# Seven-product form: another order of the first pair's products, and five operations of a head at other places of their queues

## Time and profile before

| | us |
|---|---|
| median of 3 runs (1496.05 to 1500.35) | 1499.07 |
| time of the profiled execution | 1500.38 |
| span of its profile | 1498.7 |
| PE busy in the span | 1364.2 (91%) |
| DVE, ACT, POOL busy | 972.7, 664.5, 604.8 |

### The profile page before, as it was taken

One profiled execution on the slowest core, in us unless ns is written; L12 is line 12 of the kernel. 1 busy time (PEld: TensorE's weight loads), 2 busy tenths in 40 slices (PEclk: granted clock), 3 DMA queues, 4 the chain that ended last, 5 costly groups with the idle time before them and its releaser, 6 DMA issues.

```text
span 1498.7 us, 18769 instructions
## 1 busy us (share of the span) xinstructions
PE 1364.2 (91%) x7159; PEld 1105.7 (74%) x7159; DVE 972.7 (65%) x1637; ACT 664.5 (44%) x959; POOL 604.8 (40%) x393
## 2 busy tenths in 40 slices
PE   6898999999999999988996789899999999997897
PEld 4687887888888888877874567677776767775685
DVE  6487778878696978674357266666666666667313
ACT  6244444352535353532235345555455555546113
POOL 6443333243242333253127954445455544521120
PEclk9999999999999999999997899999999999998999
DMA  6110111101011111030222111121111112002502
GB/s 186 54 43 15 29 36 36 36 22 50 22 37 34 36 29 36 29 113 11 89 66 117 28 29 36 36 64 36 43 28 43 36 35 63 23 29 99 183 28 113
DMA packets 101660, 77.82 MB, mean 52 GB/s; under 512 B 2898, under 2 KB 92099, under 8 KB 101571
## 3 DMA queue, kind: packets, MB, share of 16 engines
q1 hardware_dynamic: 101570, 76.62, 17.0%
HBM read 59.83 MB, written 16.78 MB: 51 GB/s over the span
## 4 chain that ended last, share of the span: by engine, by line
PE 66%; DVE 19%; ACT 5%; POOL 4%; issue 3%; DMA 1%; POOLq 0%; SPq 0%; DVEq 0%; ACTq 0%; PEldq 0%
PE psum L446 27%; PE psum L574 14%; PE psum L2110 3%; DVE stick L1750 3%; DVE terms L1619 3%; PE psum L2084 3%; PE psum L2028 2%; PE psum L1973 2%; PE psum L2043 2%; PE psum L1998 2%; PE psum L2019 1%; PE psum L2097 1%; DVE soft L1743 1%; POOL acc L923 1%; PE psum L1982 1%
## 5 line engine op out<-in xcount | busy, mean ns | idle before, releaser
L446 PE MATMUL psum<-u_hi,w_hi 128*128 128x512 f32 x752 | 308.7, 411 | 24.4 <-DVE u_lo L1336 6.7
L446 PE MATMUL psum<-u_lo,w_hi 128*128 128x512 f32 x752 | 306.4, 407 | 0.0
L446 PE MATMUL psum<-u_hi,w_lo 128*128 128x512 f32 x752 | 301.6, 401 | 0.0
L416 POOL TENSOR_TENSOR w_lo<-w_raw,w_hi 128x1024 fp32r<-128x1024 f32 (+1 forms) x51 | 122.7, 2406 | 325.8 <-ACT w_hi L411 325.8
L446 PEld LDWEIGHTS psum<-u_hi,w_hi 128*128 128x128 f32 x752 | 143.5, 191 | 58.1 <-issue 16.3
L446 PEld LDWEIGHTS psum<-u_lo,w_hi 128*128 128x128 f32 x752 | 143.4, 191 | 29.8 <-issue 3.8
L446 PEld LDWEIGHTS psum<-u_hi,w_lo 128*128 128x128 f32 x752 | 143.1, 190 | 29.3 <-issue 2.2
L878 POOL TENSOR_TENSOR Lb<-dec,level 128x512 f32<-128x512 f32 (+1 forms) x64 | 89.0, 1405 | 126.3 <-PE psum L2028 69.0
L574 PE MATMUL psum<-u_hi,w_hi 128*128 128x512 f32 x256 | 107.9, 421 | 22.2 <-ACT b_raw L1246 10.1
L411 ACT ACTIVATE w_hi<-w_raw 128x1024 fp32r<-128x1024 f32 (+1 forms) x51 | 52.2, 1024 | 160.5 <-PE psum L446 104.1
L1396 DVE TENSOR_TENSOR b_raw<-b_raw,psum 128x512 f32<-128x512 f32 x80 | 54.8, 684 | 102.6 <-PE psum L574 102.0
(11 more groups left out here) (257 smaller groups left out, 3050.7 us busy)
## 6 DMA issues: line engine op xcount, KB each, us to landing
w_raw<-in_a_w_in SPq DMA_DIRECT2D x33, 512.0 KB, 4.0
w_raw<-in_b_w_in SPq DMA_DIRECT2D x16, 512.0 KB, 4.9
w_raw_b<-in_b_w_in SPq DMA_DIRECT2D x16, 512.0 KB, 4.9
x_stage<-in_x SPq DMA_DIRECT2D x8, 512.0 KB, 7.3
w_raw<-in_b_w_out SPq DMA_DIRECT2D x8, 512.0 KB, 4.0
out<-fin_o SPq DMA_DIRECT2D x8, 512.0 KB, 2.6
b_rows<-o_row SPq DMA_DIRECT2D x14, 256.0 KB, 2.2
o_raw<-b_rows SPq DMA_DIRECT2D x7, 512.0 KB, 7.1
```

The costliest lines, as they stand in the source:

```text
L416: G.tensor_tensor(tiles(w_lo, key), tiles(w_raw, key), tiles(w_hi, key).bitcast(F32), ALU.subtract).then_inc(lo_done, 1)
L446: mm = PE.matmul(psum[:, half], (w_hi, w_hi, w_lo)[part][:, n % 2, k], (u_hi, u_lo, u_hi)[part][:, k, half * HALF:(half + 1) * HALF], star ...
```

## The change

1. `FIRST_ORDER` becomes p1, p5, p2, p3, p6, p7, p4. In pair 0, p5 and p3 have the second bank and the other five the first; the waits of `pair_products` and the sums in DVE's `take_pair` follow. Inputs are made in the new order: DVE makes the remainders of p3 before `sums_t` and those of p6 after it, ACT makes the upper parts of p3 before those of p6, p7 and p4. On POOL the remainders of pair 0's and 1's weights (`factor_lo`) move ahead of some of the second half's square additions, which are dealt out between them.
2. ACT, step 0 of a head: Silu of the gate, with its wait for `gn_done`, goes from step 1 behind softplus to step 0 ahead of softplus.
3. ACT, step 6: the exponential of step 7 (128 wide) goes in after the first of the three passes of the next head's softplus, instead of behind the third.
4. DVE, step 5: `scale_qk` goes from behind `exponent` to ahead of `scan`.
5. DVE, step 7: the products that end there are taken ahead of `scan`, instead of behind `exponent`.
6. DVE, step 0: `scale_v` of the first half goes ahead of `copy_aT`.

In the last head, where no pairs follow, ACT also does the split of the first output weights ahead of Silu and that of the second behind the softplus.

```diff
-FIRST_ORDER = ("p1", "p2", "p6", "p7", "p5", "p4", "p3")
+FIRST_ORDER = ("p1", "p5", "p2", "p3", "p6", "p7", "p4")
...
-            return psum[:, (p + (name in SECOND_BANK)) % 2]
+            return psum[:, (p + (name in (SECOND_BANK if p > 0 else ("p5", "p3")))) % 2]
...
         def pair_products(p, first, last):
...
+                    if p == 0 and name in ("p1", "p5"):
+                        PE.wait_ge(proj_taken, LAST_GROUP + 2 * KB - (1 if name == "p1" else 0))
+                    elif p == 0 and name in BY_ACT + ("p6",):
+                        PE.wait_ge(pair_act, 1 if name == "p2" else 2)
+                    elif p == 0:
+                        PE.wait_ge(pair_dve, {"p3": 1, "p7": 3, "p4": 4}[name])
...
         @block.gpsimd
...
             factor_lo(3)
             input_lo("p7")
+            factor_lo(4)
             input_lo("p4")
-            factor_lo(4)
+            factor_lo(5)
+            factor_sums(1)
             add_b_squares(1, 1, 4)
-            factor_sums(1)
-            factor_lo(5)
-            add_b_squares(1, 4, KB)
             factor_lo(6)
+            add_b_squares(1, 4, 5)
+            factor_lo(7)
+            add_b_squares(1, 5, 6)
+            factor_lo(8)
+            add_b_squares(1, 6, KB)
...
         @block.scalar
...
+                elif cb == HALF_KB:
+                    input_hi("p5", HALF_KB - 1)
+                    input_hi("p3", 0)
                 else:
-                    if cb == HALF_KB:
-                        input_hi("p5", HALF_KB - 1)
-                    else:
-                        for name in ("p6", "p7"):
-                            input_hi(name, cb - HALF_KB - 1)
-            for name in ("p6", "p7"):
-                input_hi(name, HALF_KB - 1)
+                    input_hi("p3", cb - HALF_KB)
             factor_hi(2)
             factor_hi(3)
             ended_pair(0)
-            for name in ("p4", "p3"):
-                for j in range(HALF_KB):
+            for j in range(HALF_KB):
+                for name in ("p6", "p7", "p4"):
                     input_hi(name, j)
+                if j == 1:
+                    ended_pair(1)
...
+            def weights(h, s):
+                w, slot = (Q_BLOCKS[s] + 1) * P, s % 2
+                arg_done.wait(act, h, s + 1)
+                A.activation(stick[:, slot, 0:w], stick[:, slot, 0:w], ACT.Exp).then_inc(a_done.handle, 1)
...
                 A.activation(soft[:, slot, 0:w], banks(bk)[:, 0:w], ACT.Abs).then_inc(soft_a.handle, 1)
+                if last_weights:
+                    weights(h - 1, NC - 1)
...
             def attend(h, follow):
                 for s in range(NC):
-                    arg_done.wait(act, h, s + 1)
-                    A.activation(stick[:, slot, 0:w], stick[:, slot, 0:w], ACT.Exp).then_inc(a_done.handle, 1)
+                    if s < NC - 1 or not follow:
+                        weights(h, s)
                     if s == 0:
                         ended_pair(14 * h + 13)
                     fill.to(STEP_AT[2 * s])
-                    if s + 2 < NC:
-                        softplus(h, s + 2)
-                    elif follow:
-                        softplus(h + 1, s + 2 - NC)
-                    if not follow and s < 2:
-                        split_hi(("out", s))
-                    if s == 1:
+                    if not follow and s == 0:
+                        split_hi(("out", 0))
+                    if s == 0:
                         gn_done.wait(act, h, 1)
                         bo_done.wait(act, h - 1, 2)
                         A.activation(b_g[:, :], b_raw[:, 2], ACT.Silu).then_inc(bg_done.handle, 1)
                         A.preload_act_table_set(LN_EXP)
+                    if s + 2 < NC:
+                        softplus(h, s + 2)
+                    elif follow:
+                        softplus(h + 1, s + 2 - NC, s == NC - 2)
+                    if not follow and s == 0:
+                        split_hi(("out", 1))
...
         @block.vector
...
-                    input_lo("p6", i - KB - HALF_KB - 1)
+                    input_lo("p3", i - KB - HALF_KB - 1)
+            input_lo("p3", HALF_KB - 1)
+            for j in range(HALF_KB):
+                sums_t(j)
+                if j > 0:
+                    input_lo("p6", j - 1)
             input_lo("p6", HALF_KB - 1)
-            for j in range(HALF_KB):
-                input_lo("p3", j)
...
             def attend(h, follow):
...
+                    if s == 5 and follow:
+                        scale_qk(h + 1)
+                    if s == NC - 1:
+                        fill.to(STEP_AT[2 * s + 1])
                     if there:
                         scan(*ahead)
-                    copy_aT(h, s, 0)
                     if s == 0:
                         scale_v(h, 0)
+                    copy_aT(h, s, 0)
                     if there:
                         exponent(*ahead)
                     fill.to(STEP_AT[2 * s + 1])
...
-                    if s == 5 and follow:
-                        scale_qk(h + 1)
```

More of the change, by code:

```diff
@@ L480, in pair_bank, with by_dve @@
         def pair_bank(p, name):
-            return psum[:, (p + (name in SECOND_BANK)) % 2]
+            return psum[:, (p + (name in (SECOND_BANK if p > 0 else ("p5", "p3")))) % 2]
+        def by_dve(p):
+            return [name for name in order_of(p) if name not in BY_ACT]
         def ring(t, f):
@@ L543, in build @@
         LO_DVE = [("p1", j) for j in range(KB // 2)] + [("p2", j) for j in range(KB // 2)] + \
-            [("p6", j) for j in range(KB // 2)] + [("p3", j) for j in range(KB // 2)]
+            [("p3", j) for j in range(KB // 2)] + [("p6", j) for j in range(KB // 2)]
         LO_POOL = [(name, j) for name in ("p5", "p7", "p4") for j in range(KB // 2)]
@@ L549, in build @@
         T_ORDER = [("p5", j) for j in range(HALF_KB)] + [(name, j) for j in range(HALF_KB) for name in ("p7", "p6", "p4")]
-        HI_ORDER = [("p1", j) for j in range(HALF_KB)] + [("p2", j) for j in range(HALF_KB)] + \
-            [("p5", j) for j in range(HALF_KB)] + [(name, j) for j in range(HALF_KB) for name in ("p6", "p7")] + \
-            [(name, j) for name in ("p4", "p3") for j in range(HALF_KB)]
+        HI_ORDER = [(name, j) for name in ("p1", "p2", "p5", "p3") for j in range(HALF_KB)] + \
+            [(name, j) for j in range(HALF_KB) for name in ("p6", "p7", "p4")]
         def pair_products(p, first, last):
@@ L564, in pair_products @@
                         PE.wait_ge(pair_dve, 5 * p + {"p7": 1, "p4": 2, "p3": 3}[name])
-                    elif p > 0:
+                    elif p == 1:
+                        PE.wait_ge(pair_dve, 2 if name == "p1" else 5)
+                    else:
                         PE.wait_ge(pair_dve, 5 * p - (1 if name == "p1" else 0))
-                    else:
-                        PE.wait_ge(proj_taken, LAST_GROUP + 2 * KB - (1 if name == "p1" else 0))
                 if p == 0 and part == 0:
@@ L958, in scale_gate @@
                 G.tensor_tensor(b_raw[:, 2], b_raw[:, 2], rsb[:, :], ALU.mult).then_inc(gn_done.handle, 1)
-            for f in range(7, FACTORS):
+            for f in range(9, FACTORS):
                 p, g = f // 7, f % 7
@@ L1256, in _ @@
             ended_pair(0)
-            for name in ("p4", "p3"):
-                for j in range(HALF_KB):
+            for j in range(HALF_KB):
+                for name in ("p6", "p7", "p4"):
                     input_hi(name, j)
-            for cb in range(HALF_KB):
+                if j == 1:
+                    ended_pair(1)
+            for cb in range(3):
                 b_square(cb, 1)
-            ended_pair(1)
-            for cb in range(HALF_KB, KB):
+            ended_pair(2)
+            for cb in range(3, KB):
                 b_square(cb, 1)
-            for f in range(2, 9):
+                if cb < 7:
+                    ended_pair(cb)
+            for f in range(7, 9):
                 ended_pair(f)
@@ L1269, in _, with softplus @@
                 ended_pair(f)
-            def softplus(h, s):
+            def weights(h, s):
+                w, slot = (Q_BLOCKS[s] + 1) * P, s % 2
+                arg_done.wait(act, h, s + 1)
+                A.activation(stick[:, slot, 0:w], stick[:, slot, 0:w], ACT.Exp).then_inc(a_done.handle, 1)
+            def softplus(h, s, last_weights=False):
                 w, slot, bk = (Q_BLOCKS[s] + 1) * P, s % 2, 2 + 2 * (s % 2)
@@ L1385, in take_pair @@
                                "p3": (one[:, after_half], one[:, after_half])}[name]
-                if name == "p6":
+                if p == 0:
+                    so_far = two[:, before] if name in ("p5", "p3") else dst
+                if name == by_dve(p)[0]:
                     dve.wait_ge(pair_act, 2 * p + 1)
@@ L1393, in take_pair @@
                 else:
-                    dve.wait_ge(pair_dve, 5 * p + BY_DVE.index(name))
+                    dve.wait_ge(pair_dve, 5 * p + by_dve(p).index(name))
```

(2 more changed lines are left out.)

8 lines of the change are left out of this document (2 added, 6 removed).

## The result

The changed kernel takes 1527.31 us (median of 4 runs, 1525.93 to 1531.43), the kernel before 1499.62 in the same comparison: ratio 1.0194, 95% interval 1.0168 to 1.0220. The profiled execution took 1526.95 us with a span of 1525.2, against 1500.38 and 1498.7 before, so the two profiles differ by 26.5.

What follows compares the result with a forecast made beforehand. PE was taken to set a head's pace, with some 5 us of holes, and pair 0 to be bound by what feeds it. -6.4 - 0.55 + 30 + 3 = +26 on 1499.07 gave 1525 us, range 1504 to 1536.

Steps and rivals of the forecast that it cites:

- pair 0, up to the norm's sums: Pair 0's new order: its last product and what follows start 6.4 us sooner, bounds 0 and -12.
- head 0: First head: POOL already ahead of the scan, p2 only 0.25 us later; -0.55 us in all.
- six heads: Heads 1 to 6: +4.2 + 1.6 - 1.4 + 0.6 = +5.0 us each, +30 together.
- last head and after: Last head: ACT waits for a remainder and the gate multiplication, Silu ahead of softplus; +3 us, between 0 and +6.
- +0.64: Step 7: PE's last product with v starts 0.64 us later, waiting for copy_aT behind p5's take and the scan.
- the hole at p2: Step 0, heads 1 to 6: PE waits 4.5 us for ACT's take of p1, behind Silu's wait for the gate.
- the clock: Heads 1 to 6: one PE restart at half clock behind the wait at p2, +1.6 us a head.
- one large term, Silu: Silu moved to step 0 delays p2 in heads 1 to 6: +4.4 us a head, restart included.
- The cover of the four additions: Pair 0's four later square additions hide behind p4 and pair 1's p1: end at 853.7, PE asks at 856.1.
- POOL first: Rival: in heads 1 to 6 POOL's gate multiplication starts before the scan; +1.7 us a head, 1505 us; chance 0.15.
- Faster: Rival: Silu's wait for the gate is covered, a head loses only -1.1 us; 1488 us; chance 0.10.
- Pair 0 gains nothing: Rival: POOL's chain in pair 0 starts 6 us later while heads cost +33; 1532 us; 0.12, within the forecast's 0.72.

Runs made afterwards that it cites:

- experiment 6: The kernel before the change with only the take of both products of step 7 moved ahead of the scan: 1521.88 us, ratio 1.0134.
- experiment 9: Experiment 7 with p5, too, taken ahead of the scan in step 7: 1493.51 us, ratio 0.9967 to the kernel before.
- experiment 4: The kernel before with pair 0's new order alone, all heads as before: 1494.65 us, ratio 0.9959.
- experiment 3: The changed kernel with the products of step 7 taken behind exponent again: 1527.88 us, ratio 1.0192 to the kernel before.
- Experiment 7: Changed kernel, but only p7 taken ahead of step 7's scan, Silu in step 1 behind p2's take, scale_qk at its old place: 1469.76 us.
- experiment 5: The changed kernel with POOL's gate multiplication one factor_lo earlier, Silu still in step 0: 1502.84 us, ratio 1.0018 to the kernel before.
- experiment 1: The changed kernel with Silu of the gate back in step 1 behind softplus: 1505.87 us, ratio 1.0041 to the kernel before.
- experiment 8: Experiment 7 with Silu in step 0, behind softplus and the take of p1: 1470.13 us, ratio 0.9791 to the kernel before.
- experiment 10: Experiment 7 with scale_qk ahead of the scan of step 5: 1471.54 us, ratio 0.9819 to the kernel before.
- experiment 11: Experiment 7 with pair 0's last and pair 1's first weight remainders ahead of the seven square additions on POOL: 1467.51 us, ratio 0.9788.
- experiment 2: The kernel before with Silu alone moved to step 0, with the last head's two output splits: 1516.94 us, ratio 1.0118.

## Why the prediction was right, and what in it was not

**The outcome.** 1527.3 lies 2.3 us from the forecast and inside the range, and the ranking of the parts by sign was right: pair 0 a small gain, the heads a large loss. By the profiles, terms forecast and measured:

| term | forecast | measured |
|---|---|---|
| pair 0, up to the norm's sums | -6.4 | -5.4 |
| head 0 | -0.55 | -1.95 |
| six heads | +30 | +31.2 |
| last head and after | +3 | +2.6 |

(Head 0's term ends at the first scores of head 1, so the wait in its step 7, forecast at +0.64, is counted with the six heads in the measured column. PE has no hole at p2 in head 0, where +0.25 was forecast, and waits 1.01 at `scale_v` instead of 1.48.)

The six heads come out right by luck: two errors, 1.4 too much and 1.3 too little a head, offset each other.

**Too large: the hole at p2.** It was forecast at 4.5 and is 3.1. The step that failed is "From the table load to the next operation ACT then needs 1040.55 - 1036.88 = 3.67 us", added behind the gate's end. From the gate's end (the multiplication starts at 1026.35 and takes 4.11, so 1030.46) to the next operation it is 2.40: the first load of 1.28 has run during the wait. I had read the earlier trace rows, where nothing waits between load and Silu, and so could not see which of the two the wait holds back.

**Too small: the clock.** It was forecast at 1.6 us a head, for one restart behind the hole at p2, and is 2.9. The step that failed is part 5's "+0.64": it counts the hole on `copy_aT` by its length, against the 1.5 and 0.8 that go, and that balance is right (3.0 measured). But it leaves out that one hole of 3.0 is charged a restart where two short ones were not, though the prediction had named the price of a restart a few lines above. The prediction expected the restart behind p2; in the changed kernel a slow stretch follows the hole in step 7 in five of the six heads, and that at p2 in three. Experiments 6 and 9 price part 5 at 22 to 24 us, where +0.64 in seven heads would be 4.5. So the prediction's picture of one large term, Silu, was half the story: parts 2 and 5 alone lengthen the span of the kernel before by 16.0 and 21.9 us.

**Added alone, the parts nearly sum; taken away, they don't.** Part 1 alone is -6.1 (experiment 4); with +16.0, +21.9 and the holes of 0.8 and 0.3 filled in seven heads, -7.7, that is +24.1 for a measured +26.5. But taking part 2 away from the change gives back 20.4 and taking part 5 away 2.6 (21.9 when it is added alone). A hole that one part fills is refilled by what another part makes late (experiment 3).

**Pair 0.** The walk forecast p2 at 816.2 (817.40), the hole ahead of p3 at 10 us until 830.6 (8.68 until 831.54), p4 at 846.1 (847.33) and the additions' end at 853.7 (854.93, by POOL's timeline). All of it is about 1 us later than forecast from p1 on (807.28 for 806.3): the chain was right. The late start is no error of the walk, since PE is 1.07 us later already in layer 0 (782.69 for 781.62). Experiment 7, with the same pair 0 and 781.54 there, starts p1 at 806.12 and the norm's sums at 856.02, 6.5 before 862.50. That is the 1.0 between -6.4 and -5.4. The cover of the four additions held, as PE asked for the sums only at 857.14.

**The rivals.** *POOL first* did not come about by itself; experiment 5 made it happen, and its total was near (1505, measured 1502.84) by another account: the gate came early enough that no hole at p2 was left (forecast +2.5), the one at `scale_v` was 0.9 and not 1.8, since the scan, started 0.97 us behind POOL, took 3.30, and the clock it had held harmless cost 0.9 a head for the hole in step 7. *Faster* is refuted by the wait of 4.2 for L973. *Pair 0 gains nothing* is refuted by experiment 4. On the table load, the Trainium skill, page "ScalarE: Activation LUTs", section "What ACT_TABLE_LOAD costs", would have had a drain on top of each load and so a longer hole at p2 than forecast; the trace has a shorter one.

**Not settled.** The prediction said that PE restarts at the half clock behind a hole of 2 us or more. Often, not always: the hole of 3.0 us in step 7 stands in seven heads of each of experiments 1, 5, 6 and 9, and by the timelines of PE 23 of these 28 are followed by a slow stretch of some 4 to 13 matmuls (7, 4, 6 and 6 of seven), 5 by none. In the changed kernel both holes of a head are, or one, or neither. What decides isn't told apart by any run here. A forecast can take the mean: 0.9 to 1.9 us of busy time a head with one such hole, 2.9 to 3.2 with two.

## What to carry to other kernels

Move an operation forward in its queue only if what it waits for will be complete by then. Taking p7, long ended, ahead of the scan was part of a gain; taking p5 there as well lost 24 us, because DVE then waits for PE's last matmul, and PE for what DVE does behind it. Count holes by their longest piece and not by their sum: about 5 us of idle time in a head cost nothing in clock when cut into five, and 0.9 us a head more when 3.0 stood together. And look at who makes what the moved operation waits for: here one place in POOL's queue was worth 24 us.

## What the runs showed of the hardware

- **A table load does not wait for its operation's semaphore.** The load ahead of Silu ran at 1025.04, its ACTIVATE at 1030.49 behind a wait of 4.17 us. So the wait hid the load's 1.28 us.
- **The size of a hole that costs clock.** None of 1.5 us or less did in these heads (before, experiments 4, 7, 8, 10, 11, all at 1.00). Those of 2.5 (experiment 3) and 2.6 (experiment 2) did in all six heads, those of 3.0 in most. In pair 0 of the kernel before, PE also restarts at 0.43 us from start to start behind the holes of 2.12 ahead of 845.76 and 852.49. A slow stretch is some 4 to 13 matmuls at 0.43 us from start to start, not 0.23.
- **DVE and POOL hold each other up in part, too.** The 896-wide scan took 2.09 when it had begun first, 3.30 when POOL's 2.39 us multiplication had begun 0.97 us earlier, and 4.18 when it had begun 0.08 earlier.
